# Attention by pairs of heads in a two-block transformer kernel, with transposes of an older unit issued first in each step

## The chip, the cores and the metric

The kernel is one program on one core of a Trainium2 chip. The core has a matrix engine (TensorE, PE in the profile), a vector engine (VectorE, DVE), a scalar engine (ScalarE, ACT), a general engine (GpSimd, POOL) and a sync engine (SyncE, SP) that starts transfers here. They run side by side and wait for each other on semaphores. Results of TensorE go to eight PSUM banks of 512 float32 columns; operands lie in the on-chip memory (called `mem` in the profile). The metric is the device time of one execution in microseconds (us).

## What is computed

A sequence of 512 tokens of width 1024 goes through two hybrid layers, each with three kinds of attention over 64-wide heads, and then through two blocks of another model, the first with a long convolution, the second with windowed attention, each followed by a mixture of experts. The parts that the change touches, cut from the reference:

```python
# hybrid layer, Q_BLOCK = 128, four query blocks; keys 0..q1 of each block
# kind 0: differential attention, 4 heads, each a pair of 64-wide score heads, values 128 wide
p = jax.nn.softmax(jnp.where(allowed, s, -jnp.inf), axis=-1)
w = p[:, :, 0] - lam * p[:, :, 1]
outs.append(jnp.einsum('bhqk,bhkd->bhqd', w, v[:, :, :q1]))
# kind 1: stick breaking, 8 heads
log_keep = jnp.where(strict, jax.nn.log_sigmoid(-z), 0.0)
log_rest = lax.cumsum(log_keep, axis=3, reverse=True) - log_keep
a = jnp.where(strict, jnp.exp(jax.nn.log_sigmoid(z) + log_rest), 0.0)
# kind 2: forgetting attention, 8 heads
logits = logits + cum_log_f[:, :, q0:q1, None] - cum_log_f[:, :, None, :q1]
p = jax.nn.softmax(jnp.where(causal, logits, -jnp.inf), axis=-1)
# second model, layer 1: windowed attention, 16 query heads on 4 key heads,
# 256 context keys and a band of two or three blocks of 128, with a sink
s_ctx = jnp.einsum('bqgrd,bkgd->bgrqk', q_b, k_c) * scale
s_loc = jnp.einsum('bqgrd,bkgd->bgrqk', q_b, k_b) * scale
p = sink_softmax(jnp.concatenate([s_ctx, s_loc], axis=-1), sink)
```

## The kernel before

Each engine has its own list of instructions, written out by hand in Python loops, with waits on semaphores (`wait_ge`) between them. A phase ends with a barrier (`end_phase`). The two hybrid layers are two turns of one hardware loop, so each attention line runs in both. All operands are float32 except the masks, which are bfloat16 and are added to the scores by a matmul with the identity.

`pe_attn`, `act_attn` and `dve_attn` are the attention phase of a hybrid layer. The work is a list of units `UN`: a head and one of its four query blocks `i`, so that a unit has `kw` = 128, 256, 384 or 512 keys. There are 16 units of kind 0 (two score matrices in one unit), 32 of kind 1 and 32 of kind 2. In step `s` TensorE computes the scores of unit `s` (L627, for kind 2 also the forget bias as a full float32 matmul, L631, and always the mask, L632) and then turns the weights of unit `s-3` (`LAG` = 3) by transposes through PSUM (L642). After four units of a head it multiplies the turned weights with the values (L656, called PV here). VectorE takes the row maxima (L721) for kinds 0 and 2 and makes the weights of the unit before (L733 to L750). ScalarE applies the exponential (L680) or the sigmoid twice (L674, L675) and then copies the turned weights of unit `s-3` out of PSUM (L691). Scores lie in banks 0 to 3 (two units of kind 0, or four of the others), turned weights in banks 4 and 5 by turns, and the results of PV in banks 6 and 7. The wait for the copies ahead of the transposes of unit `u` is `turned_out >= u - 1`: the copy of unit `u-1` may still be under way.

A 64-wide head uses 64 of the 128 rows of TensorE's array for its scores (rows 0 to 63 for an even head, 64 to 127 for an odd one), and for kinds 1 and 2 64 of its columns in PV. Consecutive heads are done one after the other.

`pe_sw_c`, `act_sw_c` and `dve_sw_c` are the windowed attention: 64 units of one head and one query block, scores of 512 or 640 columns (L1981, L1982, L1984, mask L1988), transposes (L2001), PV once in four units (L2018), with two buffers for scores and two for turned weights. ScalarE does the exponential (L2033), that of the sink (L2035) and the copy (L2043).

`dve_forget_sums` runs at the end of the phase ahead of the attention and prepares the forget bias.

Of the kernel before, what the change touches and what calls it, by code (L numbers as in the profile page):

```python
# [13 lines left out]
P = 128  # L14
D = 1024
KD = D // P
T = 512
# [174 lines left out]
def build(nc, a, out):  # L192

    with ExitStack() as ctx:
# [189 lines left out]
        PB3_ = hm.take(513)  # L384
        MTURN_ = hm.take(512)
        assert hm.at <= AR_END, hm.at
# [4 lines left out]
        FQ, FK = v(CT_ + 1024, 512), v(CT_ + 1536, 512)  # L391
        CUM = v(CT_ + 1024, 512, p=8)
        NCUM = M[32:40, CT_ + 1536:CT_ + 2048]
        FH = [v(CT_ + i * 512, 512) for i in range(2)]
# [5 lines left out]
        WT = [v(HT_ + i * 2048, 4, 512) for i in range(2)]  # L400
        PB = [v(HT_ + 4096 + i * 516, 513) for i in range(3)] + [v(PB3_, 513)]
        PB1 = [v(TMP_, 513), v(TMP_ + 516, 513)]
# [113 lines left out]
        def dve_forget_sums(A):  # L516
            FT = SMALLROW
            A.e.wait_ge(S["c_ready"], 1)
            tt(FT[0], FT[0], FT[1], ALU.subtract).then_inc(A.mark(), 1)

            nc.vector.memset(FQ, 0.0).then_inc(A.mark(), 1)
            A.e.wait_ge(*A.last)
            nc.vector.memset(FQ[32:40], 1.0).then_inc(A.mark(), 1)
            nc.vector.memset(FK, 1.0).then_inc(A.mark(), 1)
            A.e.wait_ge(*A.last)
            nc.vector.tensor_tensor_scan(CUM, one_col[0:8].to_broadcast([8, 512]), FT[0], 0.0, ALU.mult, ALU.add).then_inc(A.mark(), 1)
            A.e.wait_ge(*A.last)
            ts(NCUM, CUM, -1.0, None, ALU.mult).then_inc(A.mark(), 1)

# [65 lines left out]
        UN = [(kind, h, i) for kind, nh in ((0, 4), (1, 8), (2, 8)) for h in range(nh) for i in range(NQ)]  # L595
        LAG = 3
        HEADS = [(kind, h) for kind, nh in ((0, 4), (1, 8), (2, 8)) for h in range(nh)]

        def unit_banks(u):
            return (2 * (u % 2), 2 * (u % 2) + 1) if UN[u][0] == 0 else (u % 4,)  # L600

        def prev_user(u):

            for w in range(u - 1, -1, -1):
                if set(unit_banks(w)) & set(unit_banks(u)):
                    return w
            return None

        def pbuf(u, c):

            return PB[u % 4] if c == 0 else PB1[u % 2]

        def pe_attn(A):
            for s in range(len(UN) + LAG):
                if s < len(UN):
                    kind, h, i = UN[s]
                    w = prev_user(s)
                    if w is not None:
                        A.e.wait_ge(S["probs"], w + 1)
                    kw = (i + 1) * P  # L620
                    for c, bank in enumerate(unit_banks(s)):
                        if kind == 0:
                            tile, r = h, 64 * c
                        else:
                            tile, r = 4 * kind + h // 2, 64 * (h % 2)
                        o = ps[:, bank, 0:kw]
                        mm(o, QT[r:r + 64, tile, i * P:kw], KT[r:r + 64, tile, 0:kw], start=True, stop=False)  # L627
                        if kind == 2:
                            if i == 0:
                                A.e.wait_ge(S["a_ready"], h + 1)  # L630
                            mm(o, FQ[:, i * P:kw], FH[h % 2][:, 0:kw], start=False, stop=False)  # L631
                        m = mm(ps[:, bank, i * P:kw], IDB, MASK[:, kind, :], start=False, stop=True)  # L632
                    m.then_inc(A.mark("scores"), 1)
                if s >= LAG:
                    u = s - LAG
                    kind, h, i = UN[u]
# [1734 lines left out]
```

## Time and profile before

| what | value |
|---|---|
| median of 3 runs | 4038.24 us (4036.09 to 4044.68) |
| profiled execution, its own time | 4049.33 us |
| its span from first to last instruction | 4047.6 us |
| attention of the first hybrid layer | about 411 to 602 us of the span |
| attention of the second hybrid layer | about 1100 to 1292 us |
| windowed attention | about 3118 to 3339 us |
| TensorE busy | 3695.7 us (91%) |
| VectorE busy | 1302.3 us (32%) |
| ScalarE busy | 695.1 us (17%) |

A profile row of a group or of the timeline names the engine, the line of the kernel, the operation, what it writes and reads with shapes, and how many instructions it stands for. "PE" is the matmul itself and "PEld" the load of its stationary operand. A float32 matmul appears as two instructions, a transpose and a bfloat16 matmul as one. A busy TensorE is not TensorE at its peak, since the ends of matmuls are modelled and include the time in which a result drains. The granted clock (PEclk) is a share of full speed: 1.00 is 2.4 GHz and 0.50 is 1.2 GHz.

### The profile page before, as it was taken

How to read it: one execution, taken by the hardware profiler on the slowest of the kernel's cores; microseconds unless marked ns; L12 is line 12 of the kernel's file. 1: busy time of each engine (PE TensorE's matmuls, PEld its weight loads, DVE VectorE, ACT ScalarE, POOL GpSimd, SP SyncE). 2: the span in 40 equal slices, each digit the busy share in tenths (PEclk: the TensorE clock that was granted, in tenths of full speed). 3: DMA queues.
4: the chain of work that ended last, by engine and by line, in shares of the span. 5: the costliest groups of instructions: out<-in, count | busy, mean ns of one | idle time of the engine just before them, and what ended most of it. 6: DMA issues, size and time to landing. Idle time of an engine off the chain costs nothing. (4 is left out here: it accounts for less than half of the span.)

```text
span 4047.6 us, 34327 instructions
## 1 busy us (share of the span) xinstructions
PE 3695.7 (91%) x13610; PEld 1693.2 (42%) x13610; DVE 1302.3 (32%) x2647; ACT 695.1 (17%) x1604; POOL 0.2 (0%) x4
## 2 busy tenths in 40 slices
PE   7999999999999899898876899999989997799987
PEld 3444444344344344454654433333335553333332
DVE  1110753111175244753564112222234553111112
ACT  1000540100053111110112111111021441111111
POOL 0000000000000000000000000000000000000000
PEclk9999899999999999999968999999999999999999
DMA  3333101233300212101401477677731001699996
GB/s 136 154 137 125 42 1 63 93 125 148 143 1 1 95 50 101 47 21 48 150 28 43 173 288 284 255 282 277 303 143 63 1 1 43 243 371 356 360 372 250
DMA packets 86536, 588.11 MB, mean 145 GB/s; under 512 B 12441, under 2 KB 13372, under 8 KB 15973
## 3 DMA queue, kind: packets, MB, share of 16 engines
q1 hardware_dynamic: 78624, 572.56, 36.5%
q10 hardware_dynamic: 7748, 13.30, 1.0%
q8 instruction: 112, 1.84, 0.2%
q14 instruction: 52, 0.42, 0.0%
HBM read 583.73 MB, written 2.10 MB: 145 GB/s over the span
## 5 line engine op out<-in xcount | busy, mean ns | idle before, releaser
L428 PE MATMUL ps<-mem 128*128 128x512 f32 x1152 | 506.9, 599 | 16.9 <-DVE mem L537 16.9
L1645 PE MATMUL ps<-mem 128*64 128x512 f32 x2048 | 476.7, 608 | 43.6 <-DMA mem<-in_moe_w 23.5
L428 PEld LDWEIGHTS ps<-mem 128*128 128x128 f32 x1152 | 219.2, 192 | 301.2 <-issue 298.1
L1645 PEld LDWEIGHTS ps<-mem 128*64 128x64 f32 x2048 | 144.6, 139 | 337.8 <-issue 334.3
L1002 PE MATMUL ps<-mem 128*128 128x512 f32 (+1 forms) x768 | 251.3, 489 | 7.7 <-ACT mem L856 7.7
L1614 DVE SCALAR_TENSOR_TENSOR mem<-ps,mem 128x512 f32<-128x512 f32 x128 | 96.1, 751 | 412.6 <-PE ps L1574 409.9
L1002 PEld LDWEIGHTS ps<-mem 128*128 128x128 f32 x768 | 146.0, 191 | 113.2 <-issue 102.1
L627 PE MATMUL ps<-mem 64*128 64x256 f32 (+3 forms) x384 | 174.3, 537 | 13.2 <-POOLq L173 12.4
L774 PE MATMUL ps<-mem 128*128 128x512 f32 x384 | 167.1, 592 | 0.0
L425 PE MATMUL ps<-mem 128*128 128x512 f32 x384 | 167.0, 594 | 0.0
L1269 PE MATMUL ps<-mem 128*128 128x512 f32 (+1 forms) x384 | 142.5, 533 | 6.4 <-POOLq L173 6.4
L489 ACT ACTIVATE mem<-ps 128x512 f32<-128x512 f32 x48 | 28.7, 598 | 688.1 <-PE ps L428 688.1
L1574 PE MATMUL ps<-mem 128*128 128x512 f32 x256 | 139.9, 638 | 1.9 <-ACT mem L1601 1.4
L1669 PE MATMUL ps<-mem 128*64 128x512 f32 x512 | 125.2, 609 | 12.0 <-issue 12.0
L1556 PE MATMUL ps<-mem 128*128 128x256 f32 x512 | 121.9, 393 | 15.3 <-DMA mem<-in_k_pair 15.3
L550 DVE COPY mem<-ps 128x512 f32<-128x512 f32 x36 | 24.9, 693 | 330.0 <-PE ps L428 178.2
L1689 PE MATMUL ps<-mem 128*64 128x512 f32 x512 | 116.9, 598 | 8.3 <-issue 8.3
L1657 PE MATMUL ps<-mem 128*32 128x512 f32 x1024 | 123.1, 598 | 0.0
L1556 PEld LDWEIGHTS ps<-mem 128*128 128x128 f32 x512 | 97.2, 194 | 48.4 <-DMA mem<-in_k_pair 15.5
L1791 DVE TENSOR_TENSOR mem<-mem,ps 128x256 f32<-128x256 f32 x64 | 27.0, 421 | 278.4 <-ACT mem L1746 278.4
L425 PEld LDWEIGHTS ps<-mem 128*128 128x128 f32 x384 | 72.4, 190 | 94.0 <-issue 94.0
L774 PEld LDWEIGHTS ps<-mem 128*128 128x128 f32 x384 | 72.7, 189 | 92.4 <-issue 92.4
(287 smaller groups left out, 4278.5 us busy)
## 6 DMA issues: line engine op xcount, KB each, us to landing
mem<-in_moe_w SPq DMA_DIRECT2D x384, 1024.0 KB, 6.9
mem<-in_w_in SPq DMA_DIRECT2D x48, 1024.0 KB, 9.1
mem<-in_ada_w SPq DMA_DIRECT2D x48, 1024.0 KB, 6.7
mem<-in_hy_w_in SPq DMA_DIRECT2D x24, 1024.0 KB, 6.7
mem<-in_w_out SPq DMA_DIRECT2D x12, 1024.0 KB, 8.8
mem<-in_k_win_l SPq DMA_DIRECT2D x8, 1024.0 KB, 6.9
mem<-in_hy_w_out SPq DMA_DIRECT2D x8, 1024.0 KB, 5.8
mem<-in_sw_w_in SPq DMA_DIRECT2D x6, 1024.0 KB, 5.9
```

The source lines that it names most:

```text
L425: m = mm(ps[:, j % 4, :], HTL[:, k, t * P:(t + 1) * P], Wc[s][:, k, :], start=(k == 0), stop=(k == KD - 1))
L428: m = mm(ps[:, j % 4, :], Wc[s][:, k, t * P:(t + 1) * P], HTL[:, k, :], start=(k == 0), stop=(k == KD - 1))
L627: mm(o, QT[r:r + 64, tile, i * P:kw], KT[r:r + 64, tile, 0:kw], start=True, stop=False)
L774: m = mm(ps[:, b, :], Wr[s][:, k, b * P:(b + 1) * P], GT[:, 4 * c + k, :], start=(n == 0 and k == 0), stop=(n == 2 and k == 3))
L1002: m = mm(ps[:, j % 4, 0:L], Wc[s][:, k, (j % 4) * P:(j % 4 + 1) * P], H[:, k, :], start=(k == 0), stop=(k == KD - 1))
L1269: m = mm(ps[:, b, 0:L], Wc[s][:, k, (b % 4) * P:(b % 4 + 1) * P], src[:, k, :], start=(k == 0), stop=(k == KD - 1))
L1556: m = mm(ps[:, bank, 256 * d:256 * d + 256], HN[:, t, (2 * j + d) * P:(2 * j + d + 1) * P], SEL[:, t, 256 * i:256 * i + 256], start=(t == ...
L1574: m = mm(ps[:, bank, :], m_.YE[i % 2][:, j * P:(j + 1) * P], m_.G[i % 2], start=True, stop=True)
L1645: m = mm(ps[64 * x:64 * x + 64, pair, :], lat(k), w[x][:, k % 4, :], start=(k == 0), stop=(k == KD - 1))
L1657: m = mm(ps[r:r + CAP_C, 4, :], cxt(k), w[x][:, k % 4, :], start=(k < 2), stop=(k >= KD - 2))
L1669: m = mm(ps[64 * x:64 * x + 64, 7, :], m_.AT[:, k, :], w[x][:, k, :], start=(k == 0), stop=False)
L1689: m = mm(ps[64 * x:64 * x + 64, 7, :], m_.AT[:, k, :], w[x][:, k - 4, :], start=False, stop=(k == KD - 1))
```

## The change

In the hybrid layers a unit is now a pair of heads and a query block, for kinds 1 and 2 as it already was for kind 0: 48 units in place of 80. The two score matmuls of a pair stand next to each other, on rows 0 to 63 and 64 to 127 of the array, and so do the two PV matmuls of a pair, on columns 0 to 63 and 64 to 127. The maxima of both heads are one instruction, and so are the sigmoid and the copy. The second sigmoid of kind 1 is replaced by a subtraction of neighbours of the running product. The forget bias is a bfloat16 matmul over 72 rows (three rows of parts of the sum for each head) in place of a float32 one. The turned weights of a pair of kinds 1 and 2 fill banks 4 and 5 together. In each step the transposes of unit `s-3` (with PV) now stand ahead of the scores of unit `s`.

The windowed attention changes in the same way: 32 units of two heads, scores in banks 0 to 3 for one unit at a time, transposes two steps behind (`SLAG` = 2) and ahead of the new scores, PV for two groups side by side.

```diff
         def pe_attn(A):
             for s in range(len(UN) + LAG):
-                if s < len(UN):
-                    kind, h, i = UN[s]
-                    w = prev_user(s)
-                    if w is not None:
-                        A.e.wait_ge(S["probs"], w + 1)
...
                 if s >= LAG:
                     u = s - LAG
-                    kind, h, i = UN[u]
-                    if u >= 2:
-                        A.e.wait_ge(S["turned_out"], u - 1)
+                    kind, pair, i = UN[u]
+                    done = u - 1 if kind == 0 else u
+                    if done > 0:
+                        A.e.wait_ge(S["turned_out"], done)
                     A.e.wait_ge(S["weights"], u + 1)
...
+                if s < len(UN):
+                    kind, pair, i = UN[s]
+                    if s >= 2:
+                        A.e.wait_ge(S["probs"], s - 1)
+                    kw = (i + 1) * P
+                    b0 = 2 * (s % 2)
+                    tile = 4 * kind + pair
+                    for c in range(2):
+                        r = 64 * c
+                        mm(ps[:, b0 + c, 0:kw], QT[r:r + 64, tile, i * P:kw], KT[r:r + 64, tile, 0:kw], start=True, stop=False)
+                    if kind == 2:
+                        for c in range(2):
+                            mm(ps[:, b0 + c, 0:kw], HOTS[0:72, 2 * pair + c, :], BIAS[0:72, 0:kw], start=False, stop=False)
...
         def act_attn(A):
...
                     if kind == 1:
                         A.e.wait_ge(S["scores"], s + 1)
-                        act(pbuf(s, 0)[:, 0:kw], ps[:, bk[0], 0:kw], ACT.Sigmoid, scale=-1.0).then_inc(A.mark(), 1)
-                        act(pbuf(s, 1)[:, 0:kw], ps[:, bk[0], 0:kw], ACT.Sigmoid).then_inc(A.mark("probs"), 1)
+                        act(pset[:, :, 512 - kw:512], ps[:, b0:b0 + 2, 0:kw], ACT.Sigmoid, scale=-1.0).then_inc(A.mark("probs"), 1)
...
         def pe_sw_c(A):
-            for s in range(len(SU) + LAG):
+            for s in range(len(SU) + SLAG):
+                if s >= SLAG:
+                    u = s - SLAG
+                    g, i, rp = SU[u]
+                    nk = 2 + len(window(i))
+                    if u:
+                        A.e.wait_ge(S["turned_out"], u)
...
                 if s < len(SU):
-                    g, i, r = SU[s]
-                    if s >= 2:
-                        A.e.wait_ge(S["probs"], s - 1)
+                    g, i, rp = SU[s]
+                    if s:
+                        A.e.wait_ge(S["probs"], s)
```

TensorE's list in the attention of a hybrid layer, kind 2, three steps before. L627 is the scores, L631 the float32 bias, L632 the mask, L642 the transposes; a wait in brackets names the semaphore.

```order
L631 MATMUL ps<-mem 128x128 [waits a_ready]
L632 MATMUL ps<-mem 128x128
L642 MATMUL ps<-mem 128x128 [waits weights,turned_out]
L642 MATMUL ps<-mem 128x128
L627 MATMUL ps<-mem 128x256 [waits probs]
L631 MATMUL ps<-mem 128x256
L632 MATMUL ps<-mem 128x128
L642 MATMUL ps<-mem 128x128 [waits weights,turned_out]
L642 MATMUL ps<-mem 128x128 x2
```

The same place after, two steps. L626 is the transposes, L639 the scores, L642 the bfloat16 bias, L644 the mask.

```order
L639 MATMUL ps<-mem 128x128 [waits probs]
L639 MATMUL ps<-mem 128x128
L642 MATMUL ps<-mem 128x128 x2
L644 MATMUL ps<-mem 128x128 x2
L626 MATMUL ps<-mem 128x128 [waits weights,turned_out]
L626 MATMUL ps<-mem 128x128 x5
L639 MATMUL ps<-mem 128x256 [waits probs]
L639 MATMUL ps<-mem 128x256
```

The scores of a step now stand behind that step's transposes and their wait for the copies, and both heads' matmuls are neighbours.

ScalarE's list at the same place after. L681 is the exponential (one per head), L693 the copy of turned weights of the unit three steps older.

```order
L681 ACTIVATE mem<-ps,mem 128x256 [waits maxima,turned]
L681 ACTIVATE mem<-ps,mem 128x256
L693 ACTIVATE mem<-ps 128x2x3x128 [waits turned]
L681 ACTIVATE mem<-ps,mem 128x384 [waits maxima,turned]
L681 ACTIVATE mem<-ps,mem 128x384
L693 ACTIVATE mem<-ps 128x2x4x128 [waits turned]
```

Exponential and copy stand in the same order as before, now for two heads each.

TensorE's list in the windowed attention before: scores L1981 to L1984, mask L1988, transposes L2001, PV L2018.

```order
L1988 MATMUL ps<-mem 128x128 x2
L2001 MATMUL ps<-mem 128x128 [waits weights,i_ready,turned_out]
L2001 MATMUL ps<-mem 128x128 x4
L2018 MATMUL ps<-mem 64x512 [waits i_ready,turned_out]
L2018 MATMUL ps<-mem 64x512 x4
L1981 MATMUL ps<-mem 128x256 [waits probs]
L1982 MATMUL ps<-mem 128x256
```

And after: transposes L1985, scores L1998 and L2000, mask L2008.

```order
L1985 MATMUL ps<-mem 128x128 [waits weights,i_ready,turned_out]
L1985 MATMUL ps<-mem 128x128 x9
L1998 MATMUL ps<-mem 128x256 [waits probs]
L1998 MATMUL ps<-mem 128x256
L2000 MATMUL ps<-mem 128x256 x2
L2008 MATMUL ps<-mem 128x128 x2
```

Here too the transposes moved ahead of the scores, and the number of buffers for scores fell from two to one.

## Rows read from the trace of the kernel before

**Rows 1.** The page's second part: TensorE's busy share and granted clock, in slices.

```profile
PE   7999999999999899898876899999989997799987
PEclk9999899999999999999968999999999999999999
```

**Rows 2.** Busy time by stretch: us, PE, PEld, DVE, ACT, POOL, then PEclk, DMA, GB/s.

```profile
411.00:443.00 32.00, 31.62 (x69) 13.44 (x69) 15.08 (x45) 11.74 (x38) 0.00 (x0) 0.51 0.15 62
443.00:466.00 23.00, 22.91 (x95) 11.52 (x94) 18.55 (x54) 12.64 (x41) 0.00 (x0) 1.00 0.00 0
466.00:520.00 54.00, 53.80 (x229) 25.74 (x228) 45.72 (x103) 35.12 (x97) 0.00 (x0) 1.00 0.00 1
520.00:602.00 82.00, 80.56 (x326) 40.44 (x324) 41.63 (x116) 32.99 (x100) 0.00 (x0) 1.00 0.00 1
1100.40:1291.60 191.20, 188.92 (x712) 91.17 (x712) 121.10 (x317) 92.51 (x275) 0.00 (x0) 0.92 0.03 11
3118.20:3339.40 221.20, 206.58 (x848) 117.60 (x848) 124.54 (x414) 97.80 (x257) 0.00 (x0) 0.92 0.03 10
```

**Rows 3.** Groups by shape: line, engine, operation, count, busy us, mean ns, idle before.

```profile
L721 DVE TENSOR_REDUCE mem<-ps 128x1 f32<-128x512 f32 x32 | 21.4, 689 | 37.2 <-PE ps L632 37.2
...
L721 DVE TENSOR_REDUCE mem<-ps 128x1 f32<-128x128 f32 x32 | 8.6, 289 | 44.7 <-PE ps L632 44.7
...
L680 ACT ACTIVATE mem<-ps,mem 128x512 f32<-128x512 f32 x32 | 21.9, 686 | 44.9 <-DVE mem L721 44.9
...
L680 ACT ACTIVATE mem<-ps,mem 128x128 f32<-128x128 f32 x32 | 11.6, 366 | 38.3 <-DVE mem L721 38.3
...
L691 ACT ACTIVATE mem<-ps 128x512 f32<-128x512 f32 x40 | 24.0, 599 | 0.6 <-PE ps L642 0.6
...
L691 ACT ACTIVATE mem<-ps 128x128 f32<-128x128 f32 x40 | 11.0, 275 | 0.0
```

**Rows 4.** Timeline of kind 1 in the first layer: start us, length us, engine, line.

```profile
481.99 1.12 PE L627 MATMUL ps<-mem 64*128 64x512 f32 x2
...
483.05 0.23 PE L632 MATMUL ps<-mem 128*128 128x128 bf16 x1
...
483.32 2.37 PE L656 MATMUL ps<-mem 128*64 128x512 f32 x8
...
485.62 0.48 PE L627 MATMUL ps<-mem 64*128 64x128 f32 x2
...
486.04 0.23 PE L632 MATMUL ps<-mem 128*128 128x128 bf16 x1
...
486.38 0.28 ACT L674 ACTIVATE mem<-ps 128x128 f32<-128x128 f32 x1 [1.74 <-PE ps L632]
...
488.45 0.61 PE L642 MATMUL ps<-mem 128*128 128x128 f32 x4
```

**Rows 5.** Timeline of kind 0 in the first layer, at the low clock.

```profile
419.19 2.07 PE L627 MATMUL ps<-mem 64*128 64x512 f32 x2
...
421.19 0.29 PE L632 MATMUL ps<-mem 128*128 128x128 bf16 x1
```

**Rows 6.** Timeline of the windowed attention's second unit, at full clock.

```profile
3119.47 0.70 PE L1981 MATMUL ps<-mem 64*128 64x256 f32 x2
...
3120.54 0.23 PE L1988 MATMUL ps<-mem 128*128 128x128 bf16 x1
```

**Rows 7.** Timelines of matmuls on half the rows, then on half the columns.

```profile
1724.89 4.89 PE L931 MATMUL ps<-mem 64*128 64x512 f32 x16 [0.87 <-ACT mem L1177]
...
3556.98 1.94 PE L1669 MATMUL ps<-mem 128*64 128x512 f32 x8
```

**Rows 8.** Stretches of 4 us in the windowed attention, columns as in rows 2.

```profile
3176.00:3180.00 4.00, 3.19 (x17) 2.08 (x15) 3.73 (x15) 2.90 (x8) 0.00 (x0) 0.94 0.00 0
3180.00:3184.00 4.00, 4.00 (x12) 2.21 (x11) 2.06 (x10) 1.87 (x5) 0.00 (x0) 0.50 0.00 0
```

**Rows 9.** Timeline of VectorE at the end of the phase ahead of the attention.

```profile
405.84 0.67 DVE L519 TENSOR_TENSOR mem<-mem 8x512 f32<-8x512 f32 x1
...
410.28 0.16 DVE L564 TENSOR_TENSOR mem<-mem 128x1 f32<-128x1 f32 x1
```

More of the change, by code:

```diff
@@ L592, in build @@
         RT = v(GT_ + 11 * 512, 512)
-        UN = [(kind, h, i) for kind, nh in ((0, 4), (1, 8), (2, 8)) for h in range(nh) for i in range(NQ)]
+        HEADS = [(kind, pair) for kind in range(3) for pair in range(4)]
+        UN = [(kind, pair, i) for kind, pair in HEADS for i in range(NQ)]
         LAG = 3
-        HEADS = [(kind, h) for kind, nh in ((0, 4), (1, 8), (2, 8)) for h in range(nh)]
-        def unit_banks(u):
-            return (2 * (u % 2), 2 * (u % 2) + 1) if UN[u][0] == 0 else (u % 4,)
@@ L602, in prev_user, with weights_t @@
[L602 to L611, printed above, removed]
+        def weights_t(hh):
+            if HEADS[hh][0] == 0:
+                return v(HT_ + hh % 2 * 2048, 1, 2048)
+            if hh % 2 == 0:
+                return v(HT_, 2, 2048)
+            return v(KT_, (VN_ - KT_) // 2048 + 1, 2048)[:, ::(VN_ - KT_) // 2048, :]
@@ L643, in pe_attn @@
+                    for c in range(1 if kind == 0 else 2):
+                        bank = 4 + (u % 2 if kind == 0 else c)
+                        for j in range(i + 1):
+                            m = tr(ps[:, bank, j * P:(j + 1) * P], P_SETS[u % 4][:, c, lo + j * P:lo + (j + 1) * P], IDENT)
                     m.then_inc(A.mark("turned"), 1)
@@ L645, in pe_attn @@
                         pe_pv(A, u // NQ - 1)
+                if s < len(UN):
[11 more added lines that the diff above has]
+                            mm(ps[:, b0 + c, 0:kw], HOTS[0:72, 2 * pair + c, :], BIAS[0:72, 0:kw], start=False, stop=False)
+                    for c in range(2):
+                        m = mm(ps[:, b0 + c, i * P:kw], IDB, MASK[:, kind, :], start=False, stop=True)
+                    m.then_inc(A.mark("scores"), 1)
             pe_pv(A, len(HEADS) - 1)
@@ L649, in pe_pv @@
         def pe_pv(A, hh):
-            kind, h = HEADS[hh]
+            kind, pair = HEADS[hh]
             A.e.wait_ge(S["turned_out"], NQ * (hh + 1))
@@ L706, in dve_attn @@
-            tt(HOT, IDENT[:, 0:8], IDENT[:, 32:40], ALU.add).then_inc(A.mark(), 1)
+                    g = GT[:, 4 * kind + pair, :]
+                    tt(g, ps[:, 6 + hh % 2, :], g, ALU.mult).then_inc(A.mark("o_out"), 1)
+            for pset in P_SETS:
+                nc.vector.memset(pset[:, :, 512:513], 1.0).then_inc(A.mark(), 1)
             A.e.wait_ge(*A.last)
             for s in range(len(UN) + LAG + 1):
-                if s + 3 < len(UN) and UN[s + 3][0] == 2 and UN[s + 3][2] == 0:
-                    h = UN[s + 3][1]
-                    if h >= 2:
-                        A.e.wait_ge(S["scores"], s + 3 - NQ)
-                    ts(FH[h % 2], FK, HOT[:, h:h + 1], None, ALU.mult).then_inc(A.mark("a_ready"), 1)
@@ L731, in dve_attn @@
                     A.e.wait_ge(S["probs"], u + 1)
-                    if kind == 0:
+                    if kind == 1:
+                        for c in range(2):
+                            keep = pset[:, c, 512 - kw:512][:, ::-1]
+                            nc.vector.tensor_tensor_scan(keep, keep, one_col.to_broadcast([P, kw]), 1.0, ALU.mult, ALU.mult)\
+                                .then_inc(A.mark(), 1)
+                        A.e.wait_ge(*A.last)
+                        tt(pset[:, :, 512 - kw:512], pset[:, :, 513 - kw:513], pset[:, :, 512 - kw:512], ALU.subtract)\
+                            .then_inc(A.mark("weights"), 1)
+                    else:
+                        p0, p1 = pset[:, 0, 0:kw], pset[:, 1, 0:kw]
```

315 lines of the change are left out of this document (151 added, 164 removed).

## The prediction

> **What bounds the kernel now.** I read the page's slices first: TensorE is busy nearly everywhere, in the three attention stretches too, and its granted clock is low at the start of each [rows 1]. The table by stretch then gives the stages their sizes: 191 us for the attention of a hybrid layer (411 to 602, and 191.2 again in the second layer) and 221.2 us for the windowed attention, with TensorE busy for 189 to 207 us of these and VectorE for 121 to 125 [rows 2]. Within a layer kind 0 takes 55 us, 32 of them at the low clock, kind 1 takes 54 and kind 2 takes 82 [rows 2], that is 13.75, 13.5 and 20.5 us for each of four pairs of heads. TensorE bounds these stages, and the others fit beside it. So what the change does to TensorE's work counts, but also what it does to the work that keeps TensorE supplied. The timeline of kind 1 shows how the kernel hides the others: scores of a new unit go out while ScalarE still works on older ones, and TensorE goes from scores to transposes to PV without a gap [rows 4].
>
> **What becomes cheaper.** Two matmuls on different halves of the rows run together: 16 instructions of 512 columns on 64 rows take 4.89 us, about 0.3 each with waits included, where one alone holds the array 0.43; the same on halves of the columns, 8 in 1.94 us [rows 7]. So a pair of heads costs one head's scores, and for kinds 1 and 2 one head's PV. The float32 bias (four passes, so as much as the scores) becomes one bfloat16 pass. On TensorE alone a pair of kind 2 falls from 20.5 to about 10 us.
>
> **What becomes a chain.** For kinds 1 and 2 the turned weights of a pair fill both banks, so the transposes of unit s-3 wait for the copy of unit s-4. ScalarE does that copy behind the exponential of unit s-1, which needs the maxima and the scores of unit s-1. And the scores of unit s now stand behind those transposes. Nothing is ahead any more: scores, maxima, exponential, copy, transposes, PV and the next scores follow one another, and the time of a step is their sum. In the windowed attention it is the same, since the single buffer of scores also waits for the exponential just before. TensorE's queue is blocked at the wait, with the scores behind it, and VectorE and ScalarE wait for those.
>
> **The terms, for a pair of heads (four steps) at full clock.** Scores to mask 1.06 us at 512 columns and 0.42 at 128 [rows 4], mean 0.74, so 2.96. Two masks 0.05 and 0.23 (a bfloat16 pass of 128 columns is a quarter of what the scores add for 128, which is 0.21), so 1.12. Maxima of both heads: 0.289 and 0.689 for 128 and 512 columns, so 0.134 per 128 [rows 3]; for 256, 512, 768 and 1024 columns 0.42, 0.69, 0.96, 1.22, together 3.29. Exponentials 0.366 to 0.686, eight of mean 0.526, so 4.21. A copy of both heads by the same way from 0.275 and 0.599 [rows 3] is 0.38, 0.60, 0.82, 1.03, so 2.83, and the joined sigmoid the same. Transposes: four take 0.61, of which 0.17 is the end of the last, so 0.11 each; 20 and four ends make 2.88. PV 2.30 (483.32 to 485.62). A hand-over is about 0.1 (the mask ends at 486.27 and the sigmoid starts at 486.38) [rows 4].
> Kind 1: 2.96 + 1.12 + 2.83 + 2.83 + 2.88 + 2.30 + 8 x 0.1 = 15.7 us, against 13.5 now. Kind 2: 2.96 + 1.12 + bias + 3.29 + 4.21 + 2.83 + 2.88 + 2.30 + 12 x 0.1 = 20.8 + bias. No row shows a bfloat16 matmul of more than 128 columns; by the passes it is 0.05 per 128 columns, 1.1 us for a pair, and at most as a float32 one on all rows, 5.9; I take 1.1, since the mask is of the same kind. So 21.9, against 20.5.
> Kind 0 keeps two banks by turns and is no chain at each step, but PV needs the last copy, and the new scores now stand behind it. VectorE is busy 18.55 us in 23 [rows 2], and these 23 us hold a little over two heads, so 8.7 us per head, less 0.6 for the joined maxima; once per head it runs dry for PV (2.3), scores and masks (1.3) and hand-overs and transposes (0.8). That is 12.5 us. A layer at full clock: 4 x (12.5 + 15.7 + 21.9) = 200 us.
> Windowed attention, one of 32 units: two pairs of scores 1.07 (3119.47 to 3120.54) [rows 6] and half the time another 0.32, 1.23; masks 0.34; maxima over 1024 or 1280 columns 1.36; three small operations of VectorE and ScalarE 0.6; exponentials over 512 or 640 columns, two, 1.48; copy 1.03; 8 or 10 transposes 1.16; PV of five blocks at 0.43 for each of ten instruction pairs, 4.5 in four units, 1.12; hand-overs 0.4. Together 8.7, so 279 us, against 221.
>
> **The clock.** At the low level scores to mask at 512 columns take 2.00 us [rows 5], not 1.06. I scale scores, masks, transposes, bias and PV so: a pair of kind 1 costs 7.2 us more, one of kind 2 8.3, one of kind 0 4, a windowed unit 3.3. In the trace the clock stayed low in the first 32 us of a layer, until the first PV, though TensorE was always busy, and in the windowed attention it fell behind a stretch in which TensorE still worked 3.19 us of 4 [rows 2, 8]. In the chains TensorE streams for about 7 us of 15.7 and 9 of 21.9 at full clock, and 3.5 of 8.7 in the windowed attention: less than where the clock was lost. So it will fall in each chain, come back in the dense PV, and fall again. I take the low level for 60% of the work (between 0 and all, the bounds): a layer 200 + 0.6 x 4 x 19.5 = 247, so 56 more than 191; the windowed attention 279 + 0.6 x 106 = 343, so 122 more.
>
> **The gap ahead of the attention.** VectorE's tail from 405.84 to 410.44 [rows 9] loses two fills and gains seven small operations and a write of 1024 columns; between 1 and 5 us more, I take 3 for each layer, with TensorE idle. ScalarE's table loads and the fills at the start of the phase stay beside other work, at nothing; if the cover is gone they are below 0.3 us.
>
> **Sum.** 2 x 56 + 122 + 6 = 240 us on the profiled execution of 4049.33, whose time is 11 us above the median of the runs; on the median 4038 + 240 = 4278.
>
> **A page against the change.** ScalarE's copies do not get shorter with the array shared: 0.599 us for 512 columns stays [rows 3], and they now stand in the chain. The Trainium skill, TensorEngine Tiling (Array Packing), Performance Considerations, PSUM Bottleneck, says that packing speeds up TensorE but not the emptying of PSUM, which may become the bound. The same page's Theoretical Speedup gives up to twice for dimensions of 64 and under; by that alone the engines' sums of the third rival below would hold. By the first rule it is the chain.
>
> **Rivals.** (a) The chains are there but the clock holds at 2.4 GHz. For it: in kinds 1 and 2 it never fell before [rows 2]. Against it: those were dense. 2 x (200 - 191) + (279 - 221) + 6 = 82, so 4120. (b) The clock is low throughout. For it: the first 32 us of each layer. Against it: each PV brought it back. A layer 278, the windowed attention 385: 2 x 87 + 164 + 6 = 344, so 4382. (c) Faster: the copies finish before they are needed and the engines overlap as now, so that the busiest one bounds a step. Its place is ScalarE's list, and it decides if the copy of unit s-4 is done before the scores of unit s-1. Then VectorE or TensorE gives about 8.1, 10.5 and 10.5 us per pair, with the low start 130 us a layer, and 5.2 us per windowed unit (the scores' own round), 166: 2 x -61 - 55 + 6 = -171, so 3867. Against it: the copy stands behind the exponential in ScalarE's list. (d) The pairs do not share the array, so the change does not do what it says: scores and PV double in the chain, 2.96 or 5.3 us per pair and 2.2 per unit at full clock, near 1.6 times that at the mixed clock: 2 x 4 x 13.5 x 1.6 + 32 x 2.2 x 1.6 = 285 on top, 4560. Rows 7 speak against it.
>
> **How the numbers follow.** Chain with a mixed clock 0.78, predicted 4278, its own range 4180 to 4350 (30 to 85% low, terms 5% off); (a) 0.09; (b) 0.07; (c) 0.04; (d) 0.02. The range 4150 to 4350 leaves out (b), (c), (d) and most of (a). A measurement of this kernel can tell about 0.2%, 8 us, from no change. Faster is (c), 0.04; within 0.2% 0.01; slower 0.95.
>
> **What would show it.** In the profile after: a layer's attention near 247 us and the windowed one near 343; TensorE busy clearly below its share now, with waits for ScalarE's copies (L693, L2047) as the longest ahead of its transposes; ScalarE waiting for maxima and VectorE for scores in each step; the granted clock going down and up with PV; matmuls of a pair starting together. The prediction is wrong if TensorE stays dense in kinds 1 and 2, or if the stages get shorter while the clock stays low. The forecast falls to (a) if the clock stays at 1.00 there.

## The result, and the profile after

The changed kernel takes 4262.85 us (median of 4 runs, 4253.87 to 4267.78) where the kernel before takes 4040.2 (4036.09 to 4044.68): a ratio of 1.055, 95% interval 1.0526 to 1.0571. The profiled execution has a span of 4258.0 us, 210.4 more than before; the medians differ by 223, since the profiled execution before took 11 us more than its median, and no trace shows which stage held these 11. The forecast was 4278, with a range from 4150 to 4350.

The slices of the page stand against [rows 1]. TensorE's busy share now falls in the three attention stretches (slices 5 and 6, 12 and 13, 31 to 33 of the 40), and its granted clock with it.

```profile
PE   7999659899865989898975999999996558689987
PEclk9999869999986999999967999999997668899999
```

The table by stretch answers [rows 2]: us, busy PE, PEld, DVE, ACT, POOL, then the granted clock, the DMA share and GB/s. A stretch runs from TensorE's first scores to its last PV; measured so, the kernel before took 190.3, 190.4 and 220.7 us:

```profile
411.00:601.30 190.30, 188.79 (x712) 91.13 (x712) 120.41 (x316) 92.49 (x275) 0.00 (x0) 0.92 0.03 11
...
3118.30:3339.00 220.70, 206.17 (x848) 117.55 (x848) 124.54 (x414) 97.74 (x257) 0.00 (x0) 0.91 0.03 10
```

Now the changed kernel. Below its three stages stand two pairs of kind 1, three of kind 2 and three of kind 0.

```profile
412.50:653.00 240.50, 155.62 (x680) 78.49 (x680) 100.62 (x207) 75.80 (x195) 0.00 (x0) 0.71 0.01 5
1153.70:1393.70 240.00, 154.26 (x680) 77.94 (x680) 100.53 (x207) 75.78 (x195) 0.00 (x0) 0.72 0.01 5
3224.20:3553.50 329.30, 187.29 (x848) 119.54 (x848) 108.36 (x268) 83.45 (x193) 0.00 (x0) 0.68 0.02 7
...
492.93:526.29 33.36, 21.77 (x121) 10.71 (x120) 19.76 (x27) 10.39 (x16) 0.00 (x0) 0.90 0.00 1
551.86:631.97 80.11, 47.31 (x205) 24.01 (x205) 20.75 (x51) 20.67 (x60) 0.00 (x0) 0.63 0.00 1
...
430.00:476.71 46.71, 32.86 (x128) 17.02 (x128) 25.41 (x60) 17.49 (x52) 0.00 (x0) 0.76 0.00 1
```

The loss is all there: 50.2 + 49.6 + 108.6 = 208 us of the 210. No engine has more to do; in a layer TensorE is busy for 156 us (189 before), VectorE for 101 (120) and ScalarE for 76 (92), yet the stage takes 50 us more. In 240 us none of them is busy more than two thirds of the time. The waits of the first layer say why: engine, line, what it waited for, us in total, times, longest.

```profile
ACT mem L681 <- DVE mem L716: 110.9, 29, 8.2
DVE mem L716 <- PE ps L644: 105.7, 25, 8.4
...
PE ps L626 <- ACT mem L693: 75.2, 37, 3.3
```

They form a ring: ScalarE's exponential (L681) waits for VectorE's maxima (L716), these for TensorE's mask behind the scores (L644), and TensorE's transposes (L626), with the next scores behind them, for ScalarE's copy (L693). One turn of it, from the timeline of kind 2 (start us, length us, engine, line, and in brackets the idle time before it):

```profile
596.58 1.97 PE L626 MATMUL ps<-mem 128*128 128x128 f32 x8 [2.60 <-ACT mem L693]
...
598.47 1.65 PE L639 MATMUL ps<-mem 64*128 64x384 f32 x4
...
600.06 0.82 PE L642 MATMUL ps<-mem 72*128 72x384 bf16 x2
...
601.13 0.96 DVE L716 TENSOR_REDUCE mem<-ps 128x2 f32<-128x768 f32 x1 [5.24 <-PE ps L644]
...
602.18 0.58 ACT L681 ACTIVATE mem<-ps,mem 128x384 f32<-128x384 f32 x1 [5.66 <-DVE mem L716]
...
603.31 1.02 ACT L693 ACTIVATE mem<-ps 128x1024 f32<-128x1024 f32 x1
...
604.39 0.69 PE L626 MATMUL ps<-mem 128*128 128x128 f32 x2 [3.29 <-ACT mem L693]
```

Read the starts from top to bottom: each begins where the one above ends, to about 0.1 us. (Left out are the masks, 600.67 to 601.09, and the second exponential, 602.76 to 603.33.) From transposes to transposes, 7.81 us, one link of the ring is done at a time (VectorE's scaling of older weights runs beside it). TensorE waits 3.29 of these and works the rest at the low clock: four score instructions of 384 columns take 1.65 us.

### The profile page after: what moved, and what is told of

The parts are those of the page before. It is cut to its first block and busy times, and to the rows that moved or that the text cites. A ratio compares the mean times of both kernels' runs of the same rounds, so it can differ in the third digit from the quotient of the medians.

```text
span 4258.0 us, 33380 instructions
## 1 busy us (share of the span) xinstructions
PE 3607.2 (85%) x13546; PEld 1668.0 (39%) x13546; DVE 1251.1 (29%) x2297; ACT 647.6 (15%) x1380; POOL 0.2 (0%) x4
## 5 line engine op out<-in xcount | busy, mean ns | idle before, releaser
L426 PEld LDWEIGHTS ps<-mem 128*128 128x128 f32 x1152 | 218.9, 191 | 301.2 <-issue 298.2
L626 PE MATMUL ps<-mem 128*128 128x128 f32 x400 | 86.7, 357 | 152.9 <-ACT mem L693 150.6
L998 PEld LDWEIGHTS ps<-mem 128*128 128x128 f32 x768 | 147.2, 192 | 113.5 <-issue 101.9
L1985 PE MATMUL ps<-mem 128*128 128x128 f32 x288 | 69.0, 423 | 137.6 <-ACT mem L2047 134.7
L626 PEld LDWEIGHTS ps<-mem 128*128 128x128 f32 x400 | 58.3, 179 | 169.6 <-ACT mem L693 167.0
L1552 PEld LDWEIGHTS ps<-mem 128*128 128x128 f32 x512 | 97.7, 195 | 48.7 <-DMA mem<-in_k_pair 15.4
L716 DVE TENSOR_REDUCE mem<-ps 128x2 f32<-128x256 f32 (+1 forms) x64 | 52.7, 823 | 210.9 <-PE ps L644 210.9
```

The costliest lines, as they stand in the source:

```text
L426: m = mm(ps[:, j % 4, :], Wc[s][:, k, t * P:(t + 1) * P], HTL[:, k, :], start=(k == 0), stop=(k == KD - 1))
L626: m = tr(ps[:, bank, j * P:(j + 1) * P], P_SETS[u % 4][:, c, lo + j * P:lo + (j + 1) * P], IDENT)
L998: m = mm(ps[:, j % 4, 0:L], Wc[s][:, k, (j % 4) * P:(j % 4 + 1) * P], H[:, k, :], start=(k == 0), stop=(k == KD - 1))
L1552: m = mm(ps[:, bank, 256 * d:256 * d + 256], HN[:, t, (2 * j + d) * P:(2 * j + d + 1) * P], SEL[:, t, 256 * i:256 * i + 256], start=(t == ...
```

## The experiments

All ratios are to the kernel before, run on the same chips (4038 to 4042 us in the three groups). Stage times go from the first scores to the last PV, like those above, and come from one execution each: the windowed attention, with the same code in experiments 1 and 7, took 213.5 and 209.9 us, so differences of some 4 us between runs say nothing. Line numbers shift from kernel to kernel.

**1. Scores ahead of the transposes again.** The block of each step that issues transposes and PV is moved behind the block that issues scores, in both attentions:

```
 def pe_attn(A):            # and pe_sw_c alike
     for s in range(...):
-        if s >= LAG: ...   # transposes of unit s-3, PV
         if s < len(UN): ...# scores of unit s
+        if s >= LAG: ...
```

> The changed kernel with one thing put back: in each step of both attentions TensorE issues the scores of the new unit ahead of the transposes of the older one. Pairs of heads, shared array, bfloat16 bias and ScalarE's list stay. Theory (the order makes the chain): scores(s) no longer stand behind the wait for the copy, so scores, maxima and exponential of the next unit run beside copy and transposes. A hybrid layer's attention falls from 241.5 us to about 141, the windowed one from 331.5 to about 235, and the kernel from 4263 to about 3966, under the 4040 of the kernel before. In kinds 1 and 2 the granted clock stays mostly at 1.0. Rival A (the copy itself is the price: a pair's turned weights fill both banks, so TensorE waits for the copy in any order): the transposes still wait, the layers stay above 210 us, the kernel above 4150. Rival B (the pairs as such cost, through longer operations of VectorE and ScalarE): a layer no shorter than the 191 us of before, the kernel above 4040.

Measured: 3929.61 us, ratio 0.9735 [0.9718, 0.9752].

```profile
412.20:543.80 131.60, 110.26 (x680) 59.27 (x680) 99.33 (x207) 76.77 (x195) 0.00 (x0) 0.95 0.02 10
...
3011.70:3225.20 213.50, 151.11 (x848) 99.78 (x848) 108.37 (x268) 83.40 (x193) 0.00 (x0) 0.79 0.03 11
```

VectorE and ScalarE are busy as long as in the changed kernel, to 2 us; the layer is 109 us shorter. So the order of two blocks on TensorE makes a ratio of 1.055 out of one of 0.974, and rivals A and B fall. The waits of the first layer (L642 is here the line of the transposes) show the ring gone, 27.7 for 110.9 and 7.3 for 75.2:

```profile
ACT mem L681 <- DVE mem L716: 27.7, 28, 3.1
...
PE ps L642 <- ACT mem L693: 7.3, 10, 2.0
```

**2. The ring cut on ScalarE.** TensorE's order stays; the block with the copy moves ahead of the block with the exponential in `act_attn` and `act_sw_c`.

> The changed kernel with one thing moved, on ScalarE and not on TensorE: in each step of both attentions the copy of the older unit's turned weights stands ahead of the exponential (or sigmoid) of the new one. TensorE still issues transposes ahead of scores. Theory (the chain closes through ScalarE's list: transposes wait for a copy that stands behind the exponential of the newest unit): it is broken from the other side too, so the scores follow the transposes without that wait. A hybrid layer about 160 us (from 241.5), the windowed attention about 309 (from 331.5; its single buffer of scores still waits for the exponential just before, so most of its chain stays), the kernel about 4263 - 2 x 81 - 22 = 4079. Rival (the order on TensorE alone matters, since the scores stand behind the transposes, whatever ScalarE does first): layers stay above 230 us and the kernel above 4235.

Measured: 4062.02 us, ratio 1.006 [1.0039, 1.0079]. The layers take 152.2 and 155.9 us, the windowed attention 291.0:

```profile
412.30:564.50 152.20, 123.22 (x680) 66.15 (x680) 100.36 (x207) 75.97 (x195) 0.00 (x0) 0.86 0.02 8
...
3063.10:3354.10 291.00, 181.90 (x848) 115.15 (x848) 108.36 (x268) 86.71 (x193) 0.00 (x0) 0.68 0.02 8
```

So about 86 of the 109 us a layer come back without touching TensorE's order: the ring did close through ScalarE's list, as the prediction put it against rival (c) ("the copy stands behind the exponential in ScalarE's list"). The rival, order on TensorE alone, falls. In the windowed attention, with its single buffer of scores, 38 us come back, a third of what experiment 1 gave. There the transposes (L1985) now wait for VectorE, for the copy of the fifth block of turned weights (L2095) and the scaling of the weights (L2086), which stand behind VectorE's maxima of newer scores:

```profile
PE ps L1985 <- DVE mem L2095: 56.2, 16, 3.7
PE ps L1985 <- DVE mem L2086: 47.4, 15, 3.4
```

In the changed kernel they waited 134.7 us for ScalarE's copy there and 2.9 for VectorE. Going by these waits, a second ring through VectorE takes over once the first is cut; no run cuts it.

**3. The order alone, without pairs.** The same exchange as in 1, the other way, in the kernel before.

> The kernel before with the order alone changed: in each step of both attentions TensorE issues the transposes of the older unit ahead of the scores of the new one. No pairs, no sharing. Theory (the order is the cost, with or without pairs): here transposes wait for the copy of the unit two before them, which stands behind an exponential one unit older than in the changed kernel, so a chain is closed over two steps, each with half the work of a pair. A hybrid layer goes from 191 us to about 245 at full clock and 300 with the clock that falls in gaps; the windowed one, whose fifth block's copy stands on VectorE behind the maxima of the newest scores, from 221 to 343 at full clock or more. The kernel then takes at least 4040 + 2 x 54 + 122 = 4270, with the clock 4400 to 4490. Rival (the chain needs the pair, because only there a unit fills both banks of turned weights): two banks by turns give enough room, the stages stay within 10 us of before, the kernel below 4080.

Measured: 4462.19 us, ratio 1.105 [1.1019, 1.108].

```profile
410.90:711.30 300.40, 245.62 (x712) 111.38 (x712) 120.23 (x316) 90.99 (x275) 0.00 (x0) 0.73 0.02 7
...
3346.90:3767.60 420.70, 294.40 (x848) 158.87 (x848) 125.69 (x414) 97.71 (x257) 0.00 (x0) 0.63 0.01 5
```

The rival (no chain without pairs, below 4080) is off by 380 us. With experiment 1 and the changed kernel this fills a square (us):

| | scores first | transposes first |
|---|---|---|
| single heads, hybrid layer / windowed / kernel | 190 / 221 / 4040 | 300 / 421 / 4462 |
| pairs that share the array | 132 / 214 / 3930 | 240 / 329 / 4263 |

In a hybrid layer the order costs about 110 us with and without pairs, and the pairs save about 59 us either way (190.3 - 131.6 and 300.4 - 240.5). In the windowed attention it is not so even: the order costs 200 us with single heads and 116 with pairs, and with scores first the pairs, which have one buffer of scores in place of two, save only 7 us. Where exactly the loop closes here is less sure than in the changed kernel: the waits of this layer name PV waiting for the newest copy (33.9 us in 20 waits), and in the windowed attention most of the wait ahead of the transposes (122.6 us) has no releaser in the profile. That it is the fifth block's copy is argued from the semaphores, not shown.

**4. The sharing undone, in the chain.** The three loops over a pair's heads (scores, bias, mask) become one:

```
-for c in range(2): mm(scores of head c)
-for c in range(2): mm(bias of head c)      # kind 2
-for c in range(2): mm(mask of head c)
+for c in range(2): mm(scores); mm(bias); mm(mask)
```

> The changed kernel, with the scores of a pair no longer side by side: TensorE issues scores, bias and mask of the first head, then those of the second, so the two halves of the rows are not used together (the mask takes all rows; in the windowed attention the two heads' scores follow one another, with at most the last instruction of one beside the first of the other). PV keeps its sharing. Theory (the pairs share the array, and scores stand in the chain): the second head's scores come on top, 0.64 us per unit (2.6 per pair of four) at full clock and 1.6 times that at the mixed clock, so about 12 x 4.1 = 50 us more per hybrid layer and 32 x 1.3 = 40 more in the windowed attention; the kernel 4263 + 140 = 4400. Rival (the pair's matmuls run one after the other already, so that the order doesn't matter): the stages within 5 us of the changed kernel, 4263. Other rival (scores are not in the chain): they grow by less than 10 us although TensorE is busy longer.

Measured: 4426.69 us, ratio 1.096 [1.094, 1.0984].

```profile
413.60:730.30 316.70, 236.10 (x680) 109.42 (x680) 101.44 (x207) 75.77 (x195) 0.00 (x0) 0.59 0.01 4
...
3375.80:3719.00 343.20, 201.21 (x848) 132.39 (x848) 108.37 (x268) 83.43 (x193) 0.00 (x0) 0.65 0.02 7
```

The pairs do share the array. Apart, the scores of one head at 384 columns take as long as those of both heads in the turn above (1.65 us for `x4` at 598.47), and both stand in the ring:

```profile
700.05 1.65 PE L639 MATMUL ps<-mem 64*128 64x384 f32 x2
...
702.17 1.64 PE L639 MATMUL ps<-mem 64*128 64x384 f32 x2
```

TensorE is busy for 80 us more in a layer, part of which is the lower clock. The first layer grows by 76 us (the second by 73), not by 50. At the same time the granted clock falls further (0.71 to 0.59), though TensorE is busy for more of the time (75% for 65%); how much of the 76 that makes, no run separates. The windowed attention grows by 14 and not by 40, since there no mask stands between the two heads' scores in this version, and much of the sharing was left. In the timeline of the 16 units with two local blocks the first scores of both heads still start 0.01 us apart, although the second head's stand behind all of the first's in the list. In the 16 units with three the second head starts 1.0 us behind the first (3387.68 and 3388.70), runs beside it from there, and scores to mask take 2.86 us on average for 2.17: 11 of the 14 us. So experiments 4 and 8 test the sharing in the hybrid layers, and in the windowed attention only in part.

**5. Both orders exchanged, in both attentions.**

> Both orders put the other way than in the changed kernel, in both attentions: TensorE issues scores ahead of transposes, and ScalarE copies ahead of exponentials. Alone, scores ahead gave 131 us per hybrid layer and 213 in the windowed attention; copies ahead 154 and 291. Theory (two ways to cut one chain; what is left then is each engine's own work): in the hybrid layers both together gain a little more, to about 122 us; in the windowed attention, where scores wait for the exponential just before, a copy ahead of that exponential delays it and the next scores, so it gets longer than with scores ahead alone, 225 to 240 us. The kernel 3930 - 18 + 20 = 3932. Rival (the two edits cut different chains, so their gains add): a layer near 50 us less than 131, the windowed attention near 175, the kernel below 3860.

Measured: 3917.47 us, ratio 0.970 [0.9675, 0.9726]; layers 118.8 and 118.9, windowed attention 229.7:

```profile
2987.00:3216.70 229.70, 158.64 (x848) 103.95 (x848) 108.37 (x268) 83.79 (x193) 0.00 (x0) 0.75 0.03 10
```

As expected the gains don't add (131.6 to 118.8 where each alone gave 109 and 86), and in the windowed attention a copy ahead of the exponential costs 16 us.

**6. The waits filled.** The chain stays, and TensorE is given matmuls that nobody reads, at the start of a step:

```
+if LAG <= s < len(UN) and UN[s][0] != 0:
+    A.e.wait_ge(S["probs"], s - 1)
+    for _ in range(1 if UN[s][0] == 1 else 3):
+        mm(ps[:, 2 * (s % 2), :], IDENT, VN[:, 8, :], start=True, stop=True)
```

> The changed kernel, order and chain as they are, with matmuls added whose result nobody uses (the scores overwrite it): in kinds 1 and 2 TensorE does one or three float32 matmuls of 512 columns on all rows at the start of each step, while it would wait for ScalarE's copy. They measure what the low clock costs. The windowed attention is left alone. Theory (in the chain TensorE streams too little, so its clock falls, and the low clock lengthens every TensorE link): with the waits filled the granted clock stays at 1.0 in kinds 1 and 2, and a pair of kind 2 goes from 26.5 us to about 22.5, one of kind 1 from 16.7 to about 16; a layer from 241 us to about 220, the kernel from 4263 to about 4220, although TensorE does 64 matmuls more. Rival (the waits alone are the cost, the clock follows and costs little): the added matmuls gain nothing, a layer stays at 241 us or longer, the kernel at 4263 or above.

Measured: 4209.8 us, ratio 1.042 [1.0403, 1.0445]. The first layer, then two pairs of kind 1 and three of kind 2:

```profile
412.10:624.90 212.80, 179.42 (x808) 85.67 (x808) 100.62 (x207) 75.72 (x195) 0.00 (x0) 0.92 0.02 6
...
490.01:520.01 30.00, 25.71 (x138) 11.75 (x137) 19.77 (x27) 10.39 (x16) 0.00 (x0) 1.00 0.00 1
541.36:606.53 65.17, 61.69 (x277) 29.01 (x276) 20.75 (x51) 20.65 (x60) 0.00 (x0) 1.00 0.00 1
```

More work, and 28 us less for a layer. At a clock of 1.00 a pair of kind 1 takes 15.0 us and one of kind 2 21.7. So the low clock was 1.7 us of the 16.7 of kind 1, and at least 5.0 us of the 26.7 of kind 2: once per pair the three matmuls run past the copy, and the transposes start 0.62 us after its end and not 0.05 (552.45 in the timeline), so that the chain itself takes about 21.2 us. The other part of the loss in a chain is there at any clock. Rival (a) of the prediction supposed that the clock holds without such filling, and it did not.

**7. The best of the orders.** Scores first in both attentions, copies first in the hybrid layers alone.

> The candidate for the best version: the changed kernel with scores ahead of transposes in both attentions, and copies ahead of exponentials in the hybrid layers alone. Theory: a hybrid layer about 122 us (131 with scores ahead alone), the windowed attention 213 as there; the kernel 3930 - 18 = 3912, faster than both kernels. Rival (with scores ahead ScalarE's order no longer matters, since the copy is never what TensorE waits for): 3930, the layers at 131.

Measured: 3907.37 us, ratio 0.968 [0.9661, 0.9693]; layers 121.0 and 118.9, windowed attention 209.9:

```profile
1035.10:1154.00 118.90, 104.19 (x680) 57.34 (x680) 99.27 (x207) 75.67 (x195) 0.00 (x0) 0.98 0.03 11
...
2989.50:3199.40 209.90, 147.96 (x848) 97.12 (x848) 108.37 (x268) 83.36 (x193) 0.00 (x0) 0.80 0.03 11
```

Here a pair of kind 2 takes 9.4 us (three in the row below), where the chain took 26.7:

```profile
496.11:524.43 28.32, 28.32 (x205) 16.12 (x205) 20.76 (x52) 20.61 (x61) 0.00 (x0) 1.00 0.01 1
```

TensorE is busy without a gap: this is the "about 10 us on TensorE alone" of the prediction. This version is 3.2% faster than the kernel before and 8% faster than the changed one. Its interval overlaps that of experiment 5; what sets the two apart is the stage time of the windowed attention, 210 us for 230.

**8. What the sharing is worth without the chain.** Experiment 4's edit on top of experiment 1.

> Scores ahead of transposes in both attentions, and the scores of a pair one head after the other (bias and mask of a head behind its scores), so that they don't share the array; PV still does. It shows what the sharing is worth once the chain is gone. Theory (then TensorE's own work sets the time): the second head's scores add 0.64 us per unit, 31 us per hybrid layer at full clock of which some is hidden, so 20 to 30 us on 131; in the windowed attention 15 to 25 on 213; the kernel 3930 + 2 x 25 + 20 = 4000, still under 4040. Rival (VectorE and ScalarE bound the stages by then, so the sharing is hidden): the stages within 5 us of 131 and 213, the kernel near 3935.

Measured: 4006.57 us, ratio 0.993 [0.9905, 0.9948]; layers 166.1, windowed attention 222.6:

```profile
413.30:579.40 166.10, 161.59 (x680) 78.33 (x680) 100.79 (x207) 76.65 (x195) 0.00 (x0) 0.86 0.02 8
```

The layer grows by 34.5 us, 5 more than the upper end, with the granted clock at 0.86 for 0.95; the windowed attention by 9, where this order of the list undoes the sharing only in part, as under 4. Of the 59 us that pairs save in a layer with scores first, 34.5 hang on the sharing of the scores; the rest is with the bias in one pass, the joined operations and PV.

**9. The same filling in the windowed attention.** Two float32 matmuls of 512 columns between the exponential and the end of the copy.

> The changed kernel with matmuls added whose result nobody uses, in the hybrid layers as in the run before (one or three float32 matmuls of 512 columns on all rows at the start of a step of kinds 1 and 2), and now in the windowed attention too: two of them per unit, between the exponential and the end of ScalarE's copy, a stretch in which TensorE waits. Theory (the low clock is part of the windowed attention's price too): TensorE then streams for over 4 of 10 us in a unit, the clock stays up after a PV, and the windowed attention falls from 329 us to about 290; the hybrid layers stay at the 212.5 of the run before; the kernel at 4210 - 39 = 4171. Rival (in the windowed attention the waits alone are the cost, or two matmuls are too few to hold the clock): it stays at 329 us or gets longer by the added matmuls, up to 32 x 0.85 = 27 us.

Measured: 4230.85 us, ratio 1.047 [1.0452, 1.0493]; layers 213.2 and 214.1, the windowed attention 345.6, with a granted clock of 0.80 for 0.68:

```profile
3173.20:3518.80 345.60, 230.17 (x964) 127.70 (x964) 108.34 (x268) 83.41 (x193) 0.00 (x0) 0.80 0.02 7
```

My sum for the added work, 0.85 us for the two, was wrong. The timeline shows the added matmuls (L1980), ScalarE's copy (L2055) beside the first of them, and the transposes (L1993) that have to wait for both:

```profile
3234.26 1.02 ACT L2055 ACTIVATE mem<-ps 128x1024 f32<-128x1024 f32 x1
...
3234.41 3.61 PE L1980 MATMUL ps<-mem 128*128 128x512 f32 x4 [3.28 <-ACT mem L2047]
3237.86 1.26 PE L1993 MATMUL ps<-mem 128*128 128x128 f32 x10
...
3243.68 2.96 PE L1980 MATMUL ps<-mem 128*128 128x512 f32 x4 [3.28 <-ACT mem L2047]
```

At full clock one such matmul takes about 0.9 us (three in 2.79, in a row of experiment 6):

```profile
578.67 1.10 PE L630 MATMUL ps<-mem 128*128 128x128 f32 x8
...
580.99 2.79 PE L618 MATMUL ps<-mem 128*128 128x512 f32 x6
```

Here the two took 2.0 to 3.8 us, 3.2 on average over 29 units, since most of it ran at the low clock, and the transposes started 2.1 us after the copy's end on average, where it was 0.05 in the changed kernel. That puts about 59 us more into the ring, and the stage grew by only 16. So the clock gave back about 43 us, an estimate from these rows. TensorE's own work says the same: 230.2 us busy less 92 for the added matmuls is 138, for 187.3 at the lower clock. The low clock is thus part of the price in the windowed attention too, as the theory had it; the filling cost more than it brought.

**10. One semaphore split** (the next scores wait for the second large exponential, not for the small one behind it), on top of 7.

> The best version so far (scores ahead of transposes in both attentions, copies ahead of exponentials in the hybrid layers) with one semaphore split in the windowed attention: TensorE's next scores wait for the second large exponential of the unit before, no more for the small one (2 columns) behind it; VectorE, which needs its result, waits for that. Theory (in the windowed attention the single buffer of scores makes a ring of scores, maxima, exponentials and the next scores, and the small exponential, about 0.28 us with its hand-over, stands in it): 32 x 0.28 = 9 us less, the windowed attention about 201 us from 210, the kernel 3898 from 3907. Rival (the ring is closed by ScalarE's or VectorE's whole list, and the small exponential takes its time there in any place): no gain, 3907.

Measured: 3906.45 us, ratio 0.968 [0.9661, 0.9691]; windowed attention 209.4 us. No difference to 3907.37 that this measurement can tell. Its timeline shows the two in ScalarE's list:

```profile
3055.49 0.20 ACT L2040 ACTIVATE mem<-mem 128x2 f32<-128x2 f32 x1
3055.58 1.02 ACT L2048 ACTIVATE mem<-ps 128x1024 f32<-128x1024 f32 x1
```

The operation behind the small one starts 0.09 us after it, so at most about 3 us (32 x 0.09) stood in the ring, not 9. Once in four units the next scores wait for PV and not for ScalarE, and nothing could be gained there.

## Why the prediction was right, step by step

**The chain.** "Nothing is ahead any more": shown by the ring of waits and the turn in the timeline, and by cutting it in two places (1 and 2). Rival (c), 3867, needed the copy done before the newest scores. Its total is near what experiment 7 reached, 3907, by two errors that cancel in part: its layers were 130 us (measured 121 and 119), its windowed attention 166 (210).

**The terms at full clock.** Experiment 6 measures them with the clock at 1.00: 15.0 us for kind 1 (forecast 15.7) and 21.7, or 21.2 without the overrun of the filling, for kind 2 (21.9). The bias was taken at 1.1 us between 1.1 and 5.9, since no row showed a wide bfloat16 matmul. At full clock the row of experiment 1 is two instructions of 512 columns:

```profile
519.58 0.61 PE L627 MATMUL ps<-mem 72*128 72x512 bf16 x2
```

That is 0.44 with the end of the last (0.17) left out, or 0.05 per 128 columns and head, the lower bound.

**The clock.** A mean of 0.71 between levels of 0.5 and 1 is 58% low, and 0.68 in the windowed attention 64%; I took 60%. These are shares of time, waits included, and the 60% was of TensorE's work, so that they agree only roughly. The kinds differ: 0.90 in kind 1 is 20% low, 0.63 in kind 2 is 74%. By experiment 6 the low clock took 1.7 of the 7.2 us that kind 1 would lose at the low level throughout, 24%, and 5.0 to 5.6 of the 8.3 of kind 2, 60 to 67%. So with one share for all, kind 1 was set at 20.0 us and took 16.7, kind 2 at 26.9 and took 26.7, kind 0 at 14.9 and took 15.6. The step that failed in size is kind 1's clock. Its chain has no maxima and no exponentials of single heads, and TensorE's waits ahead of the transposes are 1.0 to 1.9 us, in kind 2 1.9 to 3.3; that the shorter waits are the reason is argued, not shown. That the whole of the forecast came so near is in part luck: one share for all was too high for kind 1, and kind 0 and the ends of the stage made up for half of that. The layer came out at 240 us, not 247.

**The windowed attention.** Forecast 343, measured 329, or 10.3 us per unit for 10.7. The 60% low was laid on PV too. But PV itself brings the clock back; one of its rows reads

```profile
3313.95 5.39 PE L2023 MATMUL ps<-mem 128*64 128x512 f32 x18
```

and at full clock (in the timeline of experiment 10) the same takes 4.51. The eight PVs of the stage take 5.38 to 6.39 us, 5.86 on average. So PV in four units loses 1.35 us to the clock, where the sum had 0.6 x 4.3 = 2.6. That is 0.3 less per unit, most of the difference of 0.4; no run assigns the rest.

**The gap ahead.** VectorE's tail, [rows 9] before, now goes from 405.58 to 411.95, 6.4 us for 4.6:

```profile
405.58 0.67 DVE L517 TENSOR_TENSOR mem<-mem 8x512 f32<-8x512 f32 x1
...
407.90 0.69 DVE L524 CAST mem<-mem 128x1024 bf16<-128x1024 f32 x1
...
411.79 0.16 DVE L570 TENSOR_TENSOR mem<-mem 128x1 f32<-128x1 f32 x1
```

So 1.8 us per layer for the 3 forecast (bounds 1 and 5). The prediction also put ScalarE's table loads below 0.3 us if they lost their cover. One takes 1.28 us (ACT_TABLE_LOAD in the timeline, before and after), and two stand inside each layer, where the kind changes; whether they lengthen a stage, no run shows.

**The sum.** 50.2 + 49.6 + 108.6 + 3.6 = 212 us for the 240 forecast (the span grew by 210, so some 2 us less went elsewhere). Of the 28 us, 12 lie in the layers, 13 in the windowed attention and 2 in the gap. In a layer kind 1 took 4 x 3.3 = 13 us less than its term and kind 2 1 less, but kind 0 took 3 more and the starts and ends, which had no term of their own, 4. Rival (b), low throughout, was wrong because PV and the dense stretches gave the clock back; (d), no sharing, because the pairs do share (4).

**ScalarE's copy.** The Trainium skill, TensorEngine Tiling (Array Packing), Performance Considerations, PSUM Bottleneck, says that packing doesn't speed up the emptying of PSUM. The runs agree in one point: emptying a pair's 1024 columns takes 1.02 us, not much less than the two copies of 512 columns before (2 x 0.599), and it was a link of the ring. But it bounds only in this order. With the orders of experiment 7 ScalarE is busy for 20.6 of 28.3 us in kind 2, and TensorE is the bound.

## What to carry to other kernels

Before blocks are exchanged in a pipelined step, write down for each engine what its next operation waits for and what stands ahead of that in the releaser's list. If this leads back to the newest unit, the step takes the sum of its links and no longer the longest of them. Less work per engine (33 us less on TensorE here) doesn't help a ring, and an exchange in one list can undo it (109 us a layer). Try a gain in work and a change of order apart: here one was worth -110 us and the other +333.

## What the runs showed of the hardware

- TensorE's granted clock fell although TensorE was never idle for longer than 3.3 us in the hybrid chain (the longest wait of L626), and in kind 1, with waits of 1.0 to 1.9 us, it was low for 20% of the time. Matmuls without a use brought a layer from 240 to 213 us (6).
- Filling a wait costs something as soon as it outlasts the wait, and it starts at the clock of that moment: two matmuls that take about 1.8 us at full clock took 2.0 to 3.8, beside a copy of 1.02, and the stage grew by 16 us though the granted clock rose from 0.68 to 0.80 (9).
- Scores undone from sharing lowered the granted clock from 0.71 to 0.59 while TensorE's busy share rose from 65% to 75% (4). The busy share alone doesn't foretell the clock.
- The scores of two heads on the two halves of the rows took 1.65 us together at the low clock, as long as one head's alone (4). In the windowed attention they also ran beside each other, in full or in part, where the list has all of one head's scores ahead of the other's and no matmul on all rows between them; in the hybrid layers, with the mask between, one followed the other (4).
